# A hybrid decoder block on 8 cores: the causal convolution leaves TensorE, pool sums become scans, gates are taken 1024 wide

## The chip, the cores and the metric

The program runs on the 8 NeuronCores of one Trainium2 chip. Each core computes one batch element of 2048 tokens, alone: the cores exchange nothing. The metric is the device time of the slowest core, in microseconds (us). On each core TensorE (PE), VectorE (DVE), ScalarE (ACT), GpSimd (POOL) and the DMA queues of SyncE (SP) and GpSimd each work in their own order and wait for each other by semaphores.

## What is computed

```python
h = rms_norm(x, norm_mix_pre)
proj = h @ w_in                                  # 1024 -> 4608 columns
x_lru, g_lru, x_pool, gates = split(proj, [1024, 2048, 2560])
# mixer A
x_lru = causal_depthwise_conv(x_lru, conv_w, conv_b)      # 4 taps per channel, along time
r, i = sigmoid(blockdiag(x_lru) + b)                      # 16 heads of 64x64
a = exp(-8 * r * softplus(-lam));  u = sqrt(1 - a*a) * i * x_lru
y_lru = scan(h_t = a_t h_{t-1} + u_t) * gelu(g_lru)
# mixer B, four groups of 128 channels, trailing windows 2, 4, 8, 16
p = mean of the last w tokens - token;  y_pool = (p @ w_grp) * scale
# merge, then the MLP
m = (sigmoid(gate_a) * (y_lru @ w_lru_up) + sigmoid(gate_b) * (y_pool @ w_pool_up)) @ w_o
x = x + rms_norm(m);  x = x + rms_norm(square(relu(rms_norm(x) @ w_ff1)) @ w_ff2)
```

## The kernel before

Channels lie on the 128 partitions and tokens run along the free axis. All of the normed, transposed input of a core is in `hT` (bf16, 8 blocks of 128 channels by 2048 tokens). Tokens are worked in two halves of 1024 (h = 0, 1), and a product is 128 output channels by 512 tokens: 8 matmuls of 128x512 into one of the 8 PSUM banks. The stages:

- A: 16 tiles of 128 tokens are loaded, normed and transposed. The first eight go through TensorE (L598), the other eight through a transposing DMA.
- B: the LRU. The index n runs over 16 channel blocks (8 for each half), and two blocks (n, n+1) are handled together. For each block and each 512 tokens (r = 0, 1): a product for x_lru, cast to bf16 in `xlb` (L733), the convolution, the bias and a cast (L751, L753), two block-diagonal gate matmuls (one of 128x512 each), two tanh, and one multiplication (L760). Then exp, square and sqrt on ScalarE over 1024 tokens, a multiplication (L771), the scan (L773), and the product with the gelu gate (L778).
- C: the pool, one group g at a time: two products, a scaled copy to `xp`, window sums by doubling (L818), the difference (L823). Its weights are folded first on TensorE (L792).
- D2 and D1: the merges of the pool branch (12 matmuls for 512 tokens) and of the LRU branch (16 matmuls), each for 8 output blocks and 2 halves. D1 of a half needs all of B of that half.
- E: w_o, norm, residual; then F1 and F2, the MLP (L921, L976 are matmuls of F2).

The convolution before is `conv_pair` (L709): 16 matmuls of 64x64 by 512 columns for two blocks, 4 taps by 4 quadrants, with the taps as diagonal matrices that GpSimd builds (L692, `conv_diag`). In every second block the two halves of the channels are swapped so that the four quadrants of the array are all in use.

The order on each engine isn't written by hand. Every operation is recorded with a priority, a cost and what it reads and writes; `Prog.schedule` places them one by one, and what comes out is a fixed order for each engine and a fixed place for each PSUM tile. The priorities of the stages come from constants (`PA`, `PC`, `PD2`, ...). Each engine then takes its instructions strictly in that order. GpSimd issues the weight loads (from f32 to bf16 on the way) and may have 4 of them under way: each waits for the one four places ahead. While TensorE has nothing to do in the first 48 us, `fill` puts matmuls on zeros (L1127) into the order, a fixed number in each gap.

`mm` records a group of matmuls (L544), `act` a ScalarE operation (L530), `load` a transfer (L562 on GpSimd's queue, L564 on SyncE's), `merge` one 512-token piece of D1 or D2 (L847 is its product with the gate).

## Time and profile before

| | us |
|---|---|
| Median of 3 runs (lowest 902.21) | 904.66 |
| Span of the profiled execution, slowest core | 901.8 |
| Spans of the eight cores | 896.5 to 901.8 |
| End of TensorE's last matmul, from the span's start | 896.5 |
| TensorE busy | 885.0 |
| VectorE busy | 463.8 |
| ScalarE busy | 369.6 |
| GpSimd busy | 190.7 |

The span is from the first to the last instruction of the slowest core, and the median lies 2.9 us above it. Busy time is a sum over an engine's instructions. Matmuls are pipelined: the mean duration of one (380 ns) is longer than the distance between two, so TensorE's work is counted here by that distance.

### The profile page before, as it was taken

The page shows a single profiled execution, that of the slowest core. Times are in us where ns is not written, and L with a number is a line of the kernel's source. Part 1 is how long each engine was busy: PE and PEld are TensorE (multiplying, and loading weights), DVE is VectorE, ACT ScalarE, POOL GpSimd, SP SyncE. Part 2 cuts the span into 40 slices and gives each one's busy share as a digit, 9 for nine tenths or more (in the row PEclk, how much of TensorE's full clock was granted, in tenths as well). Part 3 has the DMA queues.
Part 4 walks back from the last instruction along what each step waited for, and adds up shares of the span by engine and source line. Part 5 has one row for each costly group of instructions (what it writes and reads, how often), then busy time and mean ns, then how long its engine had stood idle before and what let it go on. Part 6 is the DMA issues. An engine that isn't in the chain of part 4 may idle for free.

```text
span 901.8 us, 13671 instructions; the slowest of 8 cores (896.5 to 901.8 us)
## 1 busy us (share of the span) xinstructions
PE 885.0 (98%) x4462; PEld 408.2 (45%) x4462; DVE 463.8 (51%) x668; ACT 369.6 (41%) x584; POOL 190.7 (21%) x305
## 2 busy tenths in 40 slices
PE   7999999999999999999999999999999999999997
PEld 5544434444444444444444444444444444444444
DVE  5559776984757766675455545111224443312122
ACT  5583867575563673442343334111113333311111
POOL 5323442313130021222233323100001212000000
PEclk9999999999999999999999999999999999999999
DMA  8984697237795399674798999921556555212231
GB/s 211 194 105 59 100 164 100 41 53 106 119 134 71 47 166 209 167 174 121 107 185 137 168 177 152 188 40 24 166 160 108 82 73 80 36 47 76 65 94 47
DMA packets 92870, 102.60 MB, mean 114 GB/s; under 512 B 29313, under 2 KB 80257, under 8 KB 92802
## 3 DMA queue, kind: packets, MB, share of 16 engines
q0 software_dynamic: 52768, 51.78, 42.3%
q1 hardware_dynamic: 40034, 49.96, 22.2%
q8 instruction: 37, 0.61, 0.3%
q14 instruction: 31, 0.25, 0.1%
HBM read 130.43 MB, written 16.78 MB: 163 GB/s over the span
## 4 chain that ended last, share of the span: by engine, by line
PE 92%; DMA 5%; DVE 1%; issue 1%; SPq 0%; DVEq 0%; POOL 0%; ACT 0%; POOLq 0%; ACTq 0%
PE pp L544 66%; PE pp L921 24%; DMA big<-wmrga 2%; DMA big<-wlru 2%; PE pp L709 1%; DMA big<-x 1%; PE pp L976 1%; DVE big L773 0%; PE pp L1127 0%; PE pp L792 0%; SPq L564 0%; DVE big L661 0%; DVE big L771 0%; DVE big L994 0%; PE pp L598 0%
## 5 line engine op out<-in xcount | busy, mean ns | idle before, releaser
L544 PE MATMUL pp<-big 128*128 128x512 bf16 x2880 | 627.9, 380 | 5.7 <-DMA big<-wlru 2.8
L544 PEld LDWEIGHTS pp<-big 128*128 128x128 bf16 x2880 | 280.2, 98 | 349.2 <-issue 17.4
L530 ACT ACTIVATE big<-pp 128x512 f32<-128x512 f32 (+4 forms) x217 | 138.9, 642 | 399.9 <-PE pp L921 185.6
L921 PE MATMUL pp<-big 128*128 128x512 bf16 x992 | 214.4, 379 | 0.0
L910 DVE SCALAR_TENSOR_TENSOR big<-pp,big 128x512 bf16<-128x512 f32 x128 | 88.2, 690 | 127.3 <-ACT big L530 127.2
L921 PEld LDWEIGHTS pp<-big 128*128 128x128 bf16 x992 | 97.1, 98 | 117.0
L530 ACT ACTIVATE big<-pp,dv 128x512 f32<-128x512 f32 x128 | 81.5, 689 | 88.7 <-PE pp L544 59.1
L949 DVE TENSOR_TENSOR big<-pp,big 128x512 f32<-128x512 f32 x31 | 21.3, 691 | 168.9 <-ACT big L530 153.4
L562 POOL DMA_DIRECT2D big<-wff x80 | 59.0, 737 | 212.1 <-PE pp L544 194.0
L530 ACT ACTIVATE big<-big 128x1024 bf16<-128x1024 f32 (+1 forms) x64 | 66.0, 1050 | 21.1 <-DVE big L884 13.5
L847 DVE SCALAR_TENSOR_TENSOR big<-big,pp 128x512 bf16<-128x512 f32 (+1 forms) x64 | 43.0, 682 | 31.0 <-PE pp L544 24.4
L530 ACT ACT_TABLE_LOAD x35 | 44.9, 1283 | 5.0 <-DVE big L609 2.8
L692 POOL TENSOR_SCALAR big<-identb,cvt 128x64 bf16<-128x64 bf16 x64 | 41.5, 674 | 8.0 <-PE pp L709 7.8
L953 POOL TENSOR_SCALAR st<-st 128x1 f32<-128x1 f32 x16 | 3.3, 207 | 160.6 <-ACT big L530 160.6
L773 DVE TENSOR_TENSOR_SCAN big<-big,hcar 128x1024 f32<-128x1024 f32 x16 | 37.0, 2339 | 0.2
L760 DVE SCALAR_TENSOR_TENSOR big<-big 128x512 f32<-128x512 f32 x32 | 22.0, 693 | 23.3 <-ACT big L530 23.3
L570 POOL TENSOR_SCALAR st<-st 128x1 f32<-128x1 f32 x40 | 12.8, 320 | 95.6 <-ACT big L530 94.8
L733 DVE CAST big<-pp 128x512 bf16<-128x512 f32 x32 | 22.0, 688 | 16.7 <-PE pp L544 16.5
L562 POOL DMA_DIRECT2D big<-wmrga x16 | 12.0, 751 | 82.0 <-PE pp L544 64.5
L572 POOL TENSOR_TENSOR st<-st,powc 128x1 f32<-128x1 f32 x40 | 27.4, 684 | 5.8 <-POOL st L570 0.3
L562 POOL DMA_DIRECT2D big<-wlru x18 | 13.9, 773 | 67.1 <-PE pp L544 52.7
L890 DVE SCALAR_TENSOR_TENSOR big<-big,st 128x1024 bf16<-128x1024 f32 x16 | 20.5, 1283 | 13.5 <-POOL st L572 13.4
(71 smaller groups left out, 388.4 us busy)
## 6 DMA issues: line engine op xcount, KB each, us to landing
big<-x SPq DMA_DIRECT2D x32, 512.0 KB, 6.6
big<-wff POOLq DMA_DIRECT2D x64, 256.0 KB, 6.0
big<-wmrga POOLq DMA_DIRECT2D x16, 512.0 KB, 9.4
x1s<-big SPq DMA_DIRECT2D x16, 512.0 KB, 4.7
big<-wff POOLq DMA_DIRECT2D x16, 512.0 KB, 9.8
big<-x1s SPq DMA_DIRECT2D x16, 512.0 KB, 5.0
out<-big SPq DMA_DIRECT2D x31, 256.0 KB, 3.1
big<-wlru POOLq DMA_DIRECT2D x14, 512.0 KB, 9.9
```

The source lines that it names most:

```text
L530: return e.activation(out=o, in_=i, func=func, **kw)
L544: ins = e.matmul(P.bank(tile, k)[:, width], lhsT=lt, rhs=rh, start=(i == 0), stop=(i == len(g) - 1))
L562: return P.add(eng, lambda e: e.dma_start(out=cut, in_=src), reads=list(reads), writes=[dst], dma=name, prio=prio, nbytes=nbytes, after=after)
L572: P.add("pool", lambda e: e.tensor_tensor(out=rs, in0=sd, in1=powc[:, 0:1], op=ALU.pow), reads=[sd, powc[:, 0:1]], writes=[rs], ns=730.0, ...
L692: ins = e.tensor_scalar(out=dst[:, k4, :], in0=identb[:, 128:192], scalar1=cvt[:, col:col + 1], scalar2=None, op0=ALU.mult)
L733: dve(lambda e, R=R, vx=vx, xl=xl: e.tensor_copy(out=xl[:, 3 + R.start:3 + R.stop], in_=P.bank(vx)), [vx], [xl[:, 3 + R.start:3 + R.stop]] ...
L760: dve(lambda e, R=R, xc=xc, I=I: e.scalar_tensor_tensor(out=I[:, R], in0=I[:, R], scalar=1.0, in1=xc, op0=ALU.add, op1=ALU.mult), [I[:, R] ...
L773: dve(lambda e, A=A, I=I, M=M, hc=hc: e.tensor_tensor_scan(out=M, data0=A, data1=I, initial=hc, op0=ALU.mult, op1=ALU.add), [A, I, hc], [M ...
L847: dve(lambda e: e.scalar_tensor_tensor(out=dst, in0=tg, scalar=1.0, in1=P.bank(vb), op0=ALU.add, op1=ALU.mult), [tg, vb], [dst], prio=pr)
L910: dve(lambda e, v=v, o=o, sq=sq: e.scalar_tensor_tensor(out=o, in0=P.bank(v), scalar=0.0, in1=sq, op0=ALU.is_gt, op1=ALU.mult), [v, sq], [ ...
L921: ins = e.matmul(P.bank(v, k0), lhsT=hid[k][:, TS], rhs=wff2[nh][k // 4][:, k % 4, :], start=(k == 0), stop=(k == 31))
L949: dve(lambda e: e.tensor_tensor(out=dst, in0=P.bank(v, k0), in1=gC[:, N], op=ALU.mult), [v, gC[:, N]], [v, dst], prio=pr)
```

## The change

The convolution leaves TensorE. A block's two products for x_lru (1024 tokens) now go to a pair of PSUM banks. ScalarE reads the pair once, with the current token's tap as scale and the bias, and writes `xc` in f32; VectorE then adds the other three taps with three scalar_tensor_tensor (L708 in the changed kernel) that read the same pair shifted by 1, 2 and 3 tokens. In the second half of the tokens three tiny operations add what reaches over the border. The cast of `xc` to bf16 goes to ScalarE for the first block of two and stays on VectorE for the second. The gate matmuls fill a pair of banks, and each tanh and the multiplication behind it is 1024 wide. The pool's windows of 8 and 16 are one running scan each, a window of 2 is one subtraction, and the copy to `xp` is 1024 wide. The very first products are cut into 256 columns. The constants that set the priorities, the order of the first weight loads, and the conditions on the loads are new; loads of the first MLP weights wait for the last x_lru product. The diagonals, `xlb` and the swap of channel halves are gone. The rest of the diff (memoised `cells`, 64-byte granules) concerns the building of the program.

```diff
-    PA = (120.0, 40.37)
-    PC = ((-10.0, 13.83), (424.04, 26.15))
-    PD2 = ((39.35, 81.22), (566.54, 90.4))
-    PD1 = (1065.62, 93.96)
-    PWO = 1125.97
-    PE0 = (1193.64, 24.22)
+    PA = (118.61, 41.34)
+    PC = ((-6.78, 6.03), (429.63, 29.43))
+    PD2 = ((39.63, 81.27), (551.87, 60.4))
+    PD1 = (1079.58, 74.66)
+    PWO = 821.54
+    PE0 = (1079.78, 13.19)
...
+    SPL = 1
+    CAST = (1, 0)
...
-    def conv_diag(n, c):
...
-    def conv_pair(n, vs, R, prio):
...
+    def conv(vx, xc, cc, h, prio):
+        tap = [cvt[:, C_CW + 4 * cc + k:C_CW + 4 * cc + k + 1] for k in range(4)]
+        halo = xhalo[:, 4 * cc:4 * cc + 3]
+        act(xc, lambda: P.pair(vx), AF.Identity, reads=[vx], n=1024, scale=tap[3], bias=cvt[:, C_CONVB + cc:C_CONVB + cc + 1],
+            prio=prio)
+        for d in (1, 2, 3):
+            w = tap[3 - d]
+            dve(lambda e, d=d, w=w: e.scalar_tensor_tensor(out=xc[:, d:H], in0=P.pair(vx)[:, 0:H - d], scalar=w, in1=xc[:, d:H],
+                                                           op0=ALU.mult, op1=ALU.add), [vx, xc, w], [xc], n=1024, ns=1290.0,
+                prio=prio)
+            if h == 1:
+                dve(lambda e, d=d, w=w: e.scalar_tensor_tensor(out=xc[:, 0:d], in0=halo[:, 3 - d:3], scalar=w, in1=xc[:, 0:d],
+                                                               op0=ALU.mult, op1=ALU.add), [halo, xc, w], [xc], ns=160.0,
+                    prio=prio)
...
+    def parts(n, r):
+        return [slice(256 * i, 256 * i + 256) for i in range(2)] if n == 0 and r < SPL else [ALLW]
...
+            conv(vxs[m], xc, cc, h, pg)
+            if CAST[m]:
+                act(xb, xc, AF.Copy, n=1024, prio=pg - 1)
+            else:
+                dve(lambda e, xc=xc, xb=xb: e.tensor_copy(out=xb, in_=xc), [xc], [xb], ns=700.0, prio=pg - 1)
+            for k, dst in ((0, A), (8, I)):
+                v = Ps(2)
+                for r in range(2):
+                    mm([[(wab[:, k + cc, :], xb[:, 512 * r:512 * r + 512])]], [wab, xb], [(v, r, ALLW)], pg - 30, keep=0)
+                act(dst, lambda v=v: P.pair(v), AF.Tanh, reads=[v], n=1024, scale=0.5, prio=pg - 30,
+                    bias=dv[:, D_HBA + k + cc:D_HBA + k + cc + 1])
...
+            dve(lambda e: e.tensor_tensor_scan(out=src[:, 16:HW], data0=xp[:, 16:HW], data1=xp[:, 16 - w:HW - w], initial=sc,
+                                               op0=ALU.add, op1=ALU.subtract), [xp, sc], [src], ns=2290.0, prio=pr)
...
-        stage_F1(0, m, PF1[0] + PF1[1] * m)
+        stage_F1(0, m, PF1[0] + PF1[1] * m, [bmm[-1]])
```

Three places show how the order moves. The first is TensorE at the start, from the sixth group of input transposes (L598 before, L609 after) to the first long stretch of products (L544 before, L555 after); L1127 and L1132 are the matmuls on zeros. Before:

```order
L598 MATMUL pp<-identb,big 128x128 x8
L1127 MATMUL pp<-dull 128x128 x21
L544 MATMUL pp<-big 128x512 x8
L598 MATMUL pp<-identb,big 128x128 x8
L1127 MATMUL pp<-dull 128x128 x7
L709 MATMUL pp<-big 64x512 x16
L598 MATMUL pp<-identb,big 128x128 x8
L1127 MATMUL pp<-dull 128x128 x13
L544 MATMUL pp<-big 128x512 x44
```

The same place after:

```order
L1132 MATMUL pp<-dull 128x128 x45
L609 MATMUL pp<-identb,big 128x128 x8
L1132 MATMUL pp<-dull 128x128 x8
L791 MATMUL pp<-big 128x128 x8
L1132 MATMUL pp<-dull 128x128 x41
L609 MATMUL pp<-identb,big 128x128 x8
L555 MATMUL pp<-big 128x512 x16
L555 MATMUL pp<-big 128x256 x16
L555 MATMUL pp<-big 128x512 x8
L555 MATMUL pp<-big 128x256 x16
```

All eight groups of transposes and the first fold of pool weights (L791) now stand ahead of every product, where two x_lru products and a convolution stood among them.

The second is VectorE while blocks 0 and 1 end and block 2 begins. Before (L771, L773 and L778 end a block, L733 casts an x_lru product, L818, L823 and the lines behind them belong to the pool):

```order
L771 TENSOR_TENSOR big<-big 128x1024
L823 SCALAR_TENSOR_TENSOR big<-big 128x1024 [waits s_dve]
L827 TENSOR_TENSOR big<-big,icnt 128x3
L773 SCALAR_TENSOR_TENSOR big<-big,hcar 128x1024 [waits s_dve]
L829 TENSOR_TENSOR big<-big 128x3 [waits s_dve]
L733 CAST big<-pp 128x512 [waits s_pe]
L803 COPY big<-phalo 128x16 [waits s_dve]
L776 COPY hcar<-big 128x1
L778 SCALAR_TENSOR_TENSOR big<-big 128x1024
L733 CAST big<-pp 128x512 [waits s_pe]
```

After (L770, L772 and L777 are the same three steps, L708 are the three passes of block 2's convolution):

```order
L770 TENSOR_TENSOR big<-big 128x1024 [waits s_act]
L772 SCALAR_TENSOR_TENSOR big<-big,hcar 128x1024 [waits s_dve]
L708 SCALAR_TENSOR_TENSOR big<-pp,cvt,big 128x1023 [waits s_pe,s_act]
L775 COPY hcar<-big 128x1 [waits s_dve]
L777 SCALAR_TENSOR_TENSOR big<-big 128x1024
L770 TENSOR_TENSOR big<-big 128x1024 [waits s_act]
L708 SCALAR_TENSOR_TENSOR big<-pp,cvt,big 128x1022 [waits s_dve]
L772 SCALAR_TENSOR_TENSOR big<-big,hcar 128x1024 [waits s_dve]
L708 SCALAR_TENSOR_TENSOR big<-pp,cvt,big 128x1021 [waits s_dve]
```

The passes of one block's convolution are spread among the last steps of the two blocks ahead of it.

The third is GpSimd's queue around the load of w_o (`wo`; `wmrgb` are weights of D2, `wmrga` of D1, `wlru` of B). Before:

```order
L562 DMA big<-wmrgb 128x3x512 [waits s_pe,d_wmr1]
L562 DMA big<-wmrga 128x4x512 [waits s_pe,d_wmr2]
L562 DMA big<-wo 128x8x512 [waits s_dve,s_act,s_pe,d_wlru2]
L562 DMA big<-wo 128x8x512 [waits d_wlru0]
L562 DMA big<-wmrgb 128x3x512 [waits s_pe,d_wmr0]
```

After:

```order
L573 DMA big<-wlru 128x4x512 [waits s_pe,d_wlru1]
L573 DMA big<-wo 128x8x512 [waits s_dve,s_act,s_pe,d_wlru2]
L573 DMA big<-wo 128x8x512 [waits d_wmr0]
L573 DMA big<-wmrgb 128x3x512 [waits s_pe,d_wlru0]
L573 DMA big<-wmrgb 128x3x512 [waits s_pe,d_wlru1]
L573 DMA big<-wmrgb 128x3x512 [waits s_pe,d_wo0]
L573 DMA big<-wlru 128x4x512 [waits d_wo1,s_pe]
```

The load of w_o, which stood ahead of the last D2 weights, now stands ahead of the weights of the third, fourth and fifth block of the second half's D2.

## Rows read from the trace of the kernel before

**Rows 1.** Page, the chain that ended last, by engine.
```profile
PE 92%; DMA 5%; DVE 1%; issue 1%; SPq 0%; DVEq 0%; POOL 0%; ACT 0%; POOLq 0%; ACTq 0%
```

**Rows 2.** Busy us by stretch: length, PE, PEld, DVE, ACT, POOL, clock, DMA share, GB/s.
```profile
32.50:116.00 83.50, 82.45 (x439) 37.59 (x438) 60.47 (x96) 61.17 (x83) 27.22 (x40) 1.00 0.72 109
116.00:134.00 18.00, 15.91 (x89) 6.18 (x87) 15.71 (x24) 12.03 (x17) 7.91 (x10) 0.91 0.91 166
134.00:350.00 216.00, 215.15 (x1106) 95.07 (x1104) 157.17 (x206) 130.74 (x166) 47.75 (x69) 1.00 0.68 98
...
125.00:130.00 5.00, 5.00 (x19) 1.88 (x17) 4.71 (x7) 3.68 (x6) 1.02 (x2) 0.72 0.32 63
```

**Rows 3.** The chain in order of time: start us, us, what.
```profile
25.75 1.17 PE pp L1127 x21
...
32.46 9.50 PE pp L544 x44
...
44.78 0.45 PE pp L792 x8
...
124.47 8.27 PE pp L544 x30
...
184.88 28.60 PE pp L544 x132
213.48 0.99 PE pp L709 x16
...
564.91 110.51 PE pp L921 x512
```

**Rows 4.** What TensorE waited for: us in total, times, longest.
```profile
PE pp L544 <- DMA big<-wlru: 2.8, 2, 1.7
PE pp L544 <- DVE hcar L776: 2.1, 1, 2.1
```

**Rows 5.** Timeline of ScalarE and of GpSimd near the start.
```profile
23.91 1.06 ACT L530 ACTIVATE big<-big 128x1024 bf16<-128x1024 f32 x1 [0.69 <-DMA big<-x]
...
26.95 0.73 POOL L562 DMA_DIRECT2D big<-wpt  x1
```

**Rows 6.** Groups of instructions: count, busy us, mean ns of one, idle before them.
```profile
L530 ACT ACTIVATE big<-pp,dv 128x512 f32<-128x512 f32 x128 | 81.5, 689 | 88.7 <-PE pp L544 59.1 <-DVE big L850 13.9 <-DVE big L753 6.7
L530 ACT ACT_TABLE_LOAD x35 | 44.9, 1283 | 5.0 <-DVE big L609 2.8 <-DVE warm L633 1.6
...
L773 DVE TENSOR_TENSOR_SCAN big<-big,hcar 128x1024 f32<-128x1024 f32 x16 | 37.0, 2339 | 0.2
...
L751 DVE TENSOR_SCALAR big<-pp,cvt 128x512 f32<-128x512 f32 x32 | 22.8, 744 | 7.4 <-PE pp L709 7.4
L733 DVE CAST big<-pp 128x512 bf16<-128x512 f32 x32 | 22.0, 688 | 16.7 <-PE pp L544 16.5
L760 DVE SCALAR_TENSOR_TENSOR big<-big 128x512 f32<-128x512 f32 x32 | 22.0, 693 | 23.3 <-ACT big L530 23.3
...
L882 DVE SCALAR_TENSOR_TENSOR big<-pp,st,big 128x1024 f32<-128x1024 f32 x16 | 20.5, 1281 | 7.1 <-POOL st L572 7.0
L530 ACT ACTIVATE big<-pp 128x1024 bf16<-128x1024 f32 x20 | 20.5, 1023 | 28.3 <-PE pp L544 27.0 <-PE pp L792 0.9
...
L530 ACT ACTIVATE big<-big,dv 128x1024 f32<-128x1024 f32 x16 | 19.3, 1236 | 0.1
...
L753 DVE CAST big<-big 128x512 bf16<-128x512 f32 x32 | 13.4, 443 | 0.0
...
L818 DVE TENSOR_TENSOR big<-big 128x1024 f32<-128x1024 f32 x8 | 9.7, 1213 | 0.1
```

**Rows 7.** The loads of w_o, and a table load in ScalarE's timeline.
```profile
DMA to landing us min/median/max: 15.4/18.4/21.4
...
112.15 1.28 ACT L530 ACT_TABLE_LOAD   x1
113.45 1.24 ACT L530 ACTIVATE big<-big,dv 128x1024 f32<-128x1024 f32 x1
```

More of the change, by code:

```diff
@@ L698, in build_nc @@
-    LO, HI = slice(0, 64), slice(64, 128)
-    def conv_pair(n, vs, R, prio):
-        srcs = [(n, LO, LO, 0), (n, HI, HI, 0), (n + 1, LO, HI, 1), (n + 1, HI, LO, 1)]
-        def fn(e):
-            ins = None
-            for k4 in range(4):
-                for m, rows, cols, b in srcs:
-                    ins = e.matmul(P.bank(vs[b])[cols], lhsT=convd[m % 4][rows, k4, :],
-                                   rhs=xlb[m % 3][rows, R.start + k4:R.stop + k4], start=(k4 == 0), stop=(k4 == 3))
-            return ins
-        return P.add("pe", fn, reads=[convd[m % 4] for m in (n, n + 1)] +
-                     [xlb[m % 3][:, R.start:R.stop + 3] for m in (n, n + 1)], writes=vs, ns=4 * 264.0 + 60.0, prio=prio,
-                     keep=2)
+                 WLRU[c][2 * k:2 * k + 2], 524288, prio=PW0[2 * n + k], after=x_after(XW[2 * n + k]))
@@ L1035, in build_nc @@
     load_lru(1, 1)
[L1036 removed]
+    load("pool", "wab", wabs, WAB, 524288, prio=PWAB, after=x_after(XW[4]))
     for p in range(2):
```

212 lines of the change are left out of this document (100 added, 112 removed).

## The prediction

> **What bounds the kernel now.** I read four views, in this order. The chain that ended last is TensorE for 92% of the span [rows 1]. The stretches say how full that is: from 32.5 to 350 us, where the changed stages lie, TensorE is busy 313.5 of 317.5 us, VectorE 233.4 (74%) and ScalarE 203.9 (64%) [rows 2]. The chain in order of time gives the price of TensorE's work: 512 matmuls of 128x512 take 110.51 us, 0.2158 us each [rows 3]. A convolution takes 0.99 us, and the 132 matmuls ahead of one take 28.60 us, 0.11 more than 132 x 0.2158, so a convolution costs 1.10 us of TensorE in all [rows 3]. Last, TensorE's waits are few, and two of them carry the loss inside [rows 4].
>
> So the span can be added up. Matmuls of 128x512 (2880 and 992): 3872 x 0.2158 = 835.7. Sixteen convolutions: 17.6. The last output tile (64 matmuls half as wide): 6.9. Eight groups of transposes and four folds of 0.45 [rows 3]: 5.4. Together 865.6 us. By 32.46 us [rows 3] TensorE had done 16 products' matmuls (3.45), eight groups of transposes (3.6) and one convolution (1.1), so 24.3 us went by without useful work. The tail behind the last matmul is 5.3 us. What is left of 901.8 is 6.6 us, lost in the middle. The median of the runs is 2.9 us above this execution, and I add that to each result.
>
> **The change part by part.**
>
> The convolutions leave TensorE: -17.6 us. Nothing else hides them there, since the engine is full. By the Trainium skill ("TensorE: Matmul & The Clock Gate", section "Measured speedup vs the span model") four small matmuls side by side take one matmul's time plus some 4 ns for each further one; as an estimate that makes 0.91 us for the four taps and 14.6 us for sixteen, 3 us less than the rows give. The rows are of this kernel and decide.
>
> Splitting the first products adds 32 instructions, each pair of halves about 3 ns dearer than one whole: +0.1.
>
> The start. All transposes now stand ahead of the first product. The last input tile reaches ScalarE at 23.9 us [rows 5]; square, root and scaling need 3.3 us more, so its transposes could start at about 27.3. But the fold of the first pool weights and 41 matmuls on zeros stand ahead of them. The fold needs three transfers beside the first LRU weights, as many bytes as the four small weight loads of before, three of which had landed when GpSimd issued its next load at 26.95 [rows 5]; I take 26.3. Then 0.45 for the fold, 2.3 for the 41 (21 took 1.17 [rows 3]), 0.45 for the transposes: the first product starts at 29.5 us, with 4.05 us of useful work done. That is 25.45 us without work against 24.3: +1.15. Bounds: 27.5 us (-0.85), if the weights land early, and 32 us (+3.65), if they share the DMA engines badly. The other weights of blocks 0 and 1 are asked for behind these, but the pool's 16 matmuls now run first and give them 3.5 us.
>
> VectorE for one block. Before: two casts of 0.69, two additions of 0.74, two casts of 0.44 and two multiplications of 0.69, 5.1 us. After: three passes over PSUM, for which L882 is the same form (1.28, so 3.84), a cast in every second block (0.44 on average), one 1024-wide multiplication (1.21, by L818): 5.5, and 0.3 for the tiny ones [rows 6]. Sixteen blocks: +10. The pool loses 14 of 20 additions of 1.21 and gains four scans of 2.34: -8 [rows 6]. VectorE's total barely moves, and its share rises with the shorter stretch to 78%. Cost on the path: 0, and 2 us if the three passes wait behind the 2.34 us scans that stand among them. TensorE has five gelu and pool products to do meanwhile.
>
> ScalarE for one block. Before: four tanh of 0.69, 2.76 us. After: the first pass (between 1.02 and 1.24; two per-partition operands, so I take 1.24), two tanh of 1.11, and half a cast of 1.02: 4.0 us [rows 6]. Sixteen blocks: +20. The functions now alternate more often. Following the order of functions, a table has to be loaded 52 times; the same count gives 35 before, which is what the row shows [rows 6]. 17 more of 1.28: +22. The pool's wider copies give 2 back. ScalarE goes from 204 to about 244 us of some 301, 81%. It still has room, so I take 0 on the path; the upper bound is the third rival.
>
> The Trainium skill speaks against this ("ScalarE: Activation LUTs", section "What ACT_TABLE_LOAD costs"): a change of table costs 1.28 us and then a drain of about 1.38. By it the 17 would cost 45 us. The trace doesn't agree: the load at 112.15 ends at 113.43, and the next activation starts at 113.45 [rows 7].
>
> PSUM. A pair of blocks holds four of eight banks from the first x_lru product until the third pass. This is a new hold, priced in the fifth rival.
>
> What moves. The two w_o loads (15.4 and 21.4 us to landing [rows 7]) now stand in GpSimd's queue ahead of the weights of three D2 blocks of the second half. Between the last pool product, which frees their place, and the first product that needs those weights, the changed order has 37 us of TensorE work. The transfers need about 7 us for the pool's end, 21.4 for w_o and 4 for the first D2 weights: hidden, with some 4 us to spare; without that cover a few us. E's and D1's products keep their number, and the first MLP weights have over 100 us after the product that they now wait for: 0. GpSimd loses the diagonals, which were behind no wait of TensorE's: 0.
>
> The middle. Of the 6.6 us lost, 1.1 was a wait for LRU weights (2.8 less the 1.7 at the start) and 2.1 a wait for VectorE [rows 4]. Behind the latter the granted clock fell to 0.72 of full speed for five us [rows 2], and 30 matmuls took 8.27 us in place of 6.5 [rows 3]: 1.8 more. A wait of 2.1 us thus cost 3.9. These belong to the old order, but a new order planned with the same costs has its own. I take 6.6 again, with bounds of 1.5 and 15.
>
> Sum: 865.6 - 17.6 + 0.1 + 25.45 + 6.6 + 5.3 = 885.4 us of span, and with 2.9 a median of 888.3 us, 1.8% below 904.66.
>
> **The rivals.**
>
> 1. Forecast: the convolutions' time and no more. 888.3 us, its own range 885 to 892.
>
> 2. The middle is nearly clean, since other work stands where the waits were. For it: three quarters of the loss hang on two places of the old order, and VectorE keeps its load while the pool's bursts get shorter. Against: fuller ScalarE. 888.3 less 5.3 of the 6.6: 883 us.
>
> 3. ScalarE sets TensorE's pace in parts of B. For it: 81% on average, and in strict order; tanh of gates and merges, which free the banks, queue behind table loads. Against: TensorE has D1 and D2 products between. Two more stalls of the kind seen (3.9 each) give 896 us. The w_o loads, if late, act the same way and are counted here.
>
> 4. Each change of table holds ScalarE twice as long as its row says. Then it gets 22 us more, 266 of 301 (88%), and one stall more than in rival 3: 900 us. The trace speaks against it, as above; the skill's section on table loads is what would bring it about.
>
> 5. Slower than before: the four held banks. If VectorE's three passes come late, TensorE finds no free bank and stops. Each of the eight pairs of blocks can do it. With the clock each such stop costs 3.9, so from five of eight on (19.5 against 16.4 gained) the kernel is slower; with six it takes 912 us. Against: in the order other tiles of one bank go on beside the pairs.
>
> 6. The change doesn't do what it says: the small matmuls ran in time that TensorE can't use otherwise, and it only waits where they were. 904 us. Against: no wait stands beside L709 in the chain.
>
> **How the numbers follow.** Chances: forecast 0.45, rival 2 0.26, rival 3 0.21, rival 4 0.01, rival 5 0.04, rival 6 0.03. A measurement of this kernel can tell about 2% from no change; that limit is 886.6 us. Rival 2 lies below it, and about 0.3 of the forecast's own range: 0.26 + 0.14 = 0.40 for faster by over 2%. Slower by over 2% (above 922.8) needs nearly all pairs to stop: 0.01. Within 2%: 0.59. The range goes from 882, which leaves out the lower third of rival 2 (0.09), to 897, which leaves out the upper part of rival 3 and rivals 4 to 6 (0.11 and a little): 0.2 in all. The predicted time is 888.3.
>
> **What would show it.** In the changed kernel's profile: no L709 matmul; the first long run of products at 29 to 30 us; 52 table loads of 1.28; the group of L708 at 1.28 us; ScalarE near 245 us between 30 and 335; a granted clock of 1.00 there if the waits are short. TensorE's waits show the rest: several for ScalarE of 1 us and more speak for rival 3, for VectorE's L708 for rival 5, for `wmrgb` for late w_o loads, and under 2 us in all for rival 2. I am wrong if the products start past 32 us, if passes over PSUM in place take longer than L882, or if many small waits add up beyond 10 us.

## The result, and the profile after

The changed kernel takes 893.59 us (median of 4 runs, 892.9 to 893.91), the kernel before 904.38 us on the same chip. The ratio is 0.9883, 95% interval 0.9867 to 0.990: 1.2% faster, less than the 2% that I took as the limit. The forecast was 888.3 us with a range of 882 to 897. One of the four executions before (936.19 us), and some in later calls, ran 2.7 to 20% longer with the cores of one die at a lower granted clock, and ratios leave such executions out.

First the page of the changed kernel, slowest core (core 2, span 892.4 us): the chain that ended last, by engine, and three groups that answer to [rows 1] and [rows 6].

```profile
PE 85%; issue 4%; DMA 4%; DVE 3%; ACT 3%; SPq 0%; POOL 0%; DVEq 0%; ACTq 0%; POOLq 0%
...
L708 DVE SCALAR_TENSOR_TENSOR big<-pp,cvt,big 128x1023 f32<-128x1023 f32 (+2 forms) x48 | 60.9, 1277 | 10.4 <-ACT big L541 6.8
L541 ACT ACT_TABLE_LOAD x46 | 59.0, 1283 | 8.4 <-PE pp L555 3.1
...
L541 ACT ACTIVATE big<-pp,cvt 128x1024 f32<-128x1024 f32 x22 | 25.8, 1174 | 25.3 <-PE pp L555 21.9
```

The chain's share of TensorE fell from 92% to 85%: it now runs for 6% of the span over VectorE and ScalarE (1% before), and for another 4% (1% before) over gaps between an event and the next instruction (issue). No small matmul of the convolution is left. The new passes over PSUM cost 1.277 us each (forecast 1.28). The last group mixes the sixteen first passes, 1.19 to 1.21 us each in ScalarE's timeline (forecast 1.24), with six of the pool's copies at 1.09 to 1.11. There are 46 table loads where I had counted 52.

The same stretches as in [rows 2], of the changed kernel (columns as there):

```profile
32.50:116.00 83.50, 78.73 (x405) 38.83 (x412) 64.06 (x79) 66.19 (x76) 16.77 (x25) 1.00 0.72 117
116.00:134.00 18.00, 17.95 (x84) 8.13 (x84) 16.94 (x16) 15.89 (x21) 6.05 (x8) 1.00 0.93 147
134.00:350.00 216.00, 209.46 (x944) 94.47 (x963) 160.42 (x178) 153.39 (x163) 27.44 (x37) 0.98 0.69 102
```

TensorE is busy 306.1 of 317.5 us (313.5 before). ScalarE has 235.5 us of work (203.9 before, forecast about 40 more), VectorE 241.4 (233.4). TensorE, which lost work, stands idle more than it did.

What TensorE waited for, slowest core; the answer to [rows 4]:

```profile
PE pp L555 <- DVE big L854: 4.5, 2, 4.2
PE pp L555 <- ACT big L541: 3.1, 2, 2.1
...
PE pp L555 <- DVE xhalo L716: 2.0, 2, 1.0
```

Where they lie: TensorE's timeline from the first product on (start us, us, instructions, idle before and its releaser).

```profile
29.28 10.89 PE L555 MATMUL pp<-big 128*128 128x512 bf16 x67
...
89.93 3.24 PE L555 MATMUL pp<-big 128*128 128x512 bf16 x14 [1.00 <-DVE xhalo L716]
94.14 17.14 PE L555 MATMUL pp<-big 128*128 128x512 bf16 x76 [0.97 <-ACT big L541]
113.38 27.83 PE L555 MATMUL pp<-big 128*128 128x512 bf16 x126 [2.09 <-ACT big L541]
145.35 36.19 PE L555 MATMUL pp<-big 128*128 128x512 bf16 x153 [4.15 <-DVE big L854]
...
879.76 7.15 PE L983 MATMUL pp<-big 128*128 128x256 bf16 x64
```

The sum can now be read term by term. Useful work is 865.6 - 17.6 + 0.1 = 848.1 us. The first product starts at 29.28 us, with 4.05 us of useful work done: 25.2 us without work (25.45 forecast). The last matmul ends at 886.9, so the tail is 5.5 us (5.3). What is left of 892.4 is 13.6 us, lost in the middle, where I had taken 6.6. The median lies 1.2 us above this span, not 2.9. From 888.3: -0.25, +0.2, +7.0, -1.7 make 893.6. (In each execution of the changed kernels the time is 1.5 to 1.6 us above its own slowest core's span. The rest of my 2.9 was chance: which execution was traced, and a median of three. So 1.7 of the error of 7.0 was made good by luck.) The question is where 13.6 us go.

The two long waits start far away from the engines that TensorE names. The chain of the changed kernel, in order of time (start us, us, what):

```profile
103.06 8.20 DMA big<-x
...
113.38 1.08 PE pp L555 x4
...
124.15 1.28 DVE big L674
125.50 15.33 DMA big<-big
...
142.34 1.13 DVE big L777
143.48 1.14 DVE big L760
144.61 0.61 DVE big L854
...
145.35 6.40 PE pp L555 x18
```

Read it backwards from 145.35. TensorE needs a bank that L854 frees. L854 stands in VectorE's queue behind L760, L777 and a scaling of stage A (L674), and that scaling waits for its buffer, which a transposing DMA holds for 15.33 us. The timeline of VectorE has it in one row:

```profile
141.00 1.28 DVE L674 SCALAR_TENSOR_TENSOR big<-big,st 128x1024 bf16<-128x1024 f32 x1 [6.74 <-DMA big<-big]
```

The wait at 113.38 has the same shape on ScalarE: the square of tile 13 waits 2.69 us for an x tile that takes 8.20 us to land, and the tanh that TensorE needs stands behind it.

```profile
111.40 1.06 ACT L541 ACTIVATE big<-big 128x1024 bf16<-128x1024 f32 x1 [2.69 <-DMA big<-x]
...
112.45 1.25 ACT L541 ACTIVATE big<-pp,dv 128x512 f32<-128x512 f32 x2
```

Then the clock. Stretches of 2 us of the changed kernel (busy us of PE, PEld, DVE, ACT, POOL, granted clock, DMA share, GB/s):

```profile
112.00:114.00 2.00, 0.62 (x3) 0.26 (x4) 0.70 (x2) 1.98 (x5) 1.14 (x3) 1.00 1.23 220
114.00:116.00 2.00, 2.00 (x10) 0.88 (x9) 1.78 (x2) 1.99 (x2) 0.48 (x1) 1.00 1.53 78
...
144.00:146.00 2.00, 0.65 (x2) 0.29 (x3) 2.00 (x3) 0.70 (x2) 0.00 (x0) 0.50 0.95 124
```

Behind the wait of 2.09 us the clock stays at 1.00. In the wait of 4.15 us it falls to 0.50, the lower level of 1.2 GHz, and so it stays until 150 us: 4.65 us of work at half speed, 2.3 us lost. Together: 4.5 + 3.1 + 2.0 of waits, 0.3 for a small one, 2.3 for the clock are 12.2 of the 13.6 us.

All eight cores run the same program, and that is of use here. TensorE waits for L854 for 4.0 to 5.3 us on every core, for L716 2.0 to 2.2, for ScalarE between 1.2 and 3.5. Before, the spans of the eight cores had a mean of 899.5 us, now 890.5. In what follows "middle" is a core's span less 848.1, 25.2 and 5.5, which is 878.8, and its mean over the cores is 11.7 us here. (For the kernel before it is the span less 865.6, 24.3 and 5.3: 4.3 in the mean, 6.6 on the slowest core.)

### The profile page after: what moved, and what is told of

Read it like the earlier page. It is cut to its first block, busy times and chain, and to the rows that moved or that the text cites. A ratio compares the mean times of both kernels' runs of the same rounds, so it can differ in the third digit from the quotient of the medians.

```text
span 892.4 us, 13044 instructions; the slowest of 8 cores (887.7 to 892.4 us)
## 1 busy us (share of the span) xinstructions
PE 867.5 (97%) x4222; PEld 409.4 (46%) x4301; DVE 467.7 (52%) x611; ACT 402.2 (45%) x579; POOL 150.6 (17%) x241
## 4 chain that ended last, share of the span: by engine, by line
PE 85%; issue 4%; DMA 4%; DVE 3%; ACT 3%; SPq 0%; POOL 0%; DVEq 0%; ACTq 0%; POOLq 0%
PE pp L555 60%; PE pp L928 24%; ACT big L541 2%; DMA big<-x 2%; DMA big<-big 2%; PE pp L983 1%; PE pp L1132 1%; DVE big L674 1%; DVE big L826 1%; DVE big L708 0%; ACT L541 0%; DVE big L854 0%; DVE big L830 0%; SPq L575 0%; PE pp L609 0%
## 5 line engine op out<-in xcount | busy, mean ns | idle before, releaser
L555 PE MATMUL pp<-big 128*128 128x512 bf16 (+1 forms) x2853 | 622.8, 378 | 12.9 <-DVE big L854 4.5
L555 PEld LDWEIGHTS pp<-big 128*128 128x128 bf16 x2912 | 284.5, 98 | 349.8 <-issue 18.3
L928 PE MATMUL pp<-big 128*128 128x512 bf16 x972 | 213.4, 379 | 1.1
L928 PEld LDWEIGHTS pp<-big 128*128 128x128 bf16 x992 | 97.1, 98 | 117.0
L541 ACT ACTIVATE big<-big 128x1024 bf16<-128x1024 f32 (+1 forms) x72 | 75.3, 1053 | 55.0 <-DVE big L891 38.5
L541 ACT ACTIVATE big<-pp,dv 128x512 f32<-128x512 f32 (+1 forms) x96 | 76.4, 827 | 40.9 <-PE pp L555 17.7
L708 DVE SCALAR_TENSOR_TENSOR big<-pp,cvt,big 128x1023 f32<-128x1023 f32 (+2 forms) x48 | 60.9, 1277 | 10.4 <-ACT big L541 6.8
L854 DVE SCALAR_TENSOR_TENSOR big<-big,pp 128x512 bf16<-128x512 f32 (+1 forms) x64 | 42.6, 680 | 22.7 <-PE pp L555 14.9
L772 DVE TENSOR_TENSOR_SCAN big<-big,hcar 128x1024 f32<-128x1024 f32 x16 | 37.5, 2346 | 0.6
L541 ACT ACTIVATE big<-pp,cvt 128x1024 f32<-128x1024 f32 x22 | 25.8, 1174 | 25.3 <-PE pp L555 21.9
L573 POOL DMA_DIRECT2D big<-wlru x18 | 13.6, 758 | 114.9 <-PE pp L555 94.0
L581 POOL TENSOR_SCALAR st<-st 128x1 f32<-128x1 f32 x40 | 17.3, 433 | 90.0 <-ACT big L541 89.3
L897 DVE SCALAR_TENSOR_TENSOR big<-big,st 128x1024 bf16<-128x1024 f32 x16 | 20.5, 1284 | 18.7 <-POOL st L583 18.7
L960 POOL TENSOR_SCALAR st<-st 128x1 f32<-128x1 f32 x16 | 3.3, 208 | 151.7 <-ACT big L541 151.6
L760 DVE SCALAR_TENSOR_TENSOR big<-big 128x1024 f32<-128x1024 f32 x16 | 19.5, 1220 | 13.7 <-ACT big L541 13.7
L674 DVE SCALAR_TENSOR_TENSOR big<-big,st 128x1024 bf16<-128x1024 f32 x16 | 20.5, 1282 | 9.1 <-DMA big<-big 6.7
## 6 DMA issues: line engine op xcount, KB each, us to landing
big<-wff POOLq DMA_DIRECT2D x16, 512.0 KB, 10.5
```

The lines of the kernel that those rows point to most:

```text
L541: return e.activation(out=o, in_=i, func=func, **kw)
L555: ins = e.matmul(P.bank(tile, k)[:, width], lhsT=lt, rhs=rh, start=(i == 0), stop=(i == len(g) - 1))
L573: return P.add(eng, lambda e: e.dma_start(out=cut, in_=src), reads=list(reads), writes=[dst], dma=name, prio=prio, nbytes=nbytes, after=after)
L674: dve(lambda e: e.scalar_tensor_tensor(out=hb, in0=xin, scalar=rs, in1=gA1, op0=ALU.mult, op1=ALU.mult), [xin, rs, gA1], [hb], n=1024, pri ...
L708: dve(lambda e, d=d, w=w: e.scalar_tensor_tensor(out=xc[:, d:H], in0=P.pair(vx)[:, 0:H - d], scalar=w, in1=xc[:, d:H], op0=ALU.mult, op1=A ...
L772: dve(lambda e, A=A, I=I, M=M, hc=hc: e.tensor_tensor_scan(out=M, data0=A, data1=I, initial=hc, op0=ALU.mult, op1=ALU.add), [A, I, hc], [M ...
```

## Theories

**Late transfers.** Stage A's second half (tiles 8 to 15) brings transfers whose landing time varies, and each of them is waited for by a queue in strict order, ahead of work that TensorE needs. **ScalarE** (rival 3 of the prediction): table loads and passes set the pace. **Held banks** (rival 5): VectorE's passes over PSUM come late. **The price** (rival 6): TensorE's convolutions did not cost what the sum says.

e2, e4, e5, e6 and e8 leave work out or change it, as said at each, and show only times; the other kernels compute what the reference does. In nearly all kernels below each engine has the order of instructions of the kernel that they are made from; where a dependency is changed, the planner still sees the old one, and only the waits that are written out follow the new one.

## Experiments on the long waits

**A third buffer (e1).** Tiles 8 to 15 use three buffers for the scaled rows, the third in free space.

```
-    hbA = [carve(88 + 2 * s, 2, BF16) for s in range(2)]
+    hbA, trA = [carve(o, 2, BF16) for o in (88, 90, 156)], []
...
-        hb = hbA[tt % 2]
+        hb = hbA[tt % (2 if tt < 8 else 3)]
```

> The changed kernel in its own order of instructions, with one edit: tiles 8 to 15 of stage A write their scaled rows (L674) into one of three buffers in place of one of two. Transfer theory (stage A's transposing DMAs hold the buffers, VectorE waits 6.7 us at L674 with the scan's followers queued behind, TensorE waits 4.2 us and its clock falls): the wait and the slow stretch behind it go, 893.6 less 6 to 7.5 us, about 887 us, and VectorE's longest wait for a big<-big DMA is under 1 us. ScalarE theory (table loads and passes set TensorE's pace): VectorE was early anyway, less than 1.5 us gained, 892 to 894. Held-bank theory (the passes over PSUM come late): 892 to 894 too, and TensorE's wait moves to L708 or L716.

Measured: 889.8 us, ratio 0.9834 (0.9815 to 0.9852), mean of the spans 884.7. The wait for L854 is 0.3 us on seven cores and 0.8 on one. That is the wait that the edit should remove, and neither rival foresaw it. But the time fell by 4, not 6 to 7.5: two cores now lose most at 113 us, where the x tile comes later than in the run above. The slowest core (core 3), the stretch of 2 us behind the wait, and TensorE's waits:

```profile
114.00:116.00 2.00, 2.00 (x7) 0.68 (x6) 2.00 (x3) 1.97 (x3) 0.95 (x2) 0.64 1.22 208
```

```profile
PE pp L555 <- ACT big L541: 3.7, 2, 2.7
```

A wait of 2.7 us here, and the clock falls. The kernel's time is that of its slowest core, so one late x tile on one core is enough.

**No table loads (e2).**

```
-            act(A, A, AF.Exp, n=1024, scale=ch, bias=ch, prio=pc)
+            act(A, A, AF.Exp, n=1024, scale=ch, bias=ch, prio=pc, run=AF.Tanh)
...
-            act(M, M, AF.Sqrt, n=1024, scale=-1.0, bias=1.0, prio=pc)
+            act(M, M, AF.Sqrt, n=1024, scale=-1.0, bias=1.0, prio=pc, run=AF.Square)
```

> The changed kernel in its own order, but the exponentials of stage B run as tanh and its square roots as squares, so that hardly a table is loaded there (other numbers in the output, same tiles). ScalarE theory: some 35 loads of 1.28 us, 45 us of ScalarE's time, go, and with them most of the 13.6 us lost in the middle: 893.6 less 5 to 9, 885 to 889 us. Transfer theory: the loads lie beside TensorE's work, only the 2.1 us wait for ScalarE may shorten since ScalarE has caught up when the late x tile comes; the 4.2 us wait stays: 891 to 893.6 us.

Measured: 889.4 us, ratio 0.9837 (0.9822 to 0.9852), mean span 882.9. The loads fell from 46 to 4:

```profile
L541 ACT ACT_TABLE_LOAD x4 | 5.1, 1283 | 4.6 <-DVE big L620 2.4 <-DVE warm L644 1.6 <-PE pp L555 0.5
```

So 54 us less on ScalarE bought 4 us. The ScalarE theory had asked for 5 to 9. The late-transfer theory as I had put it allowed 2.6 at most: it fell here, in its pure form. The transfers still land late; the row of VectorE below, of core 4, shows a wait of 4.49 us for a transposing DMA, but now for a later tile, and TensorE waits for L854 on three cores only (1.6 to 2.3 us).

```profile
143.67 1.28 DVE L674 SCALAR_TENSOR_TENSOR big<-big,st 128x1024 bf16<-128x1024 f32 x1 [4.49 <-DMA big<-big]
```

**Short passes (e4).** Each pass of VectorE over PSUM covers 64 columns.

```
-... out=xc[:, d:H], in0=P.pair(vx)[:, 0:H - d], scalar=w, in1=xc[:, d:H],
+... out=xc[:, d:d + 64], in0=P.pair(vx)[:, 0:64], scalar=w, in1=xc[:, d:d + 64],
```

> The changed kernel in its own order, but each of the 48 passes of VectorE over a PSUM pair (L708) handles 64 columns in place of some 1022 (part of the convolution is left out). It takes about 1.1 us from each, 50 us of VectorE in all, and frees each pair of banks 3 us earlier. Held-bank theory: TensorE's waits for banks and for the cast go, 893.6 less 5 to 10, 884 to 888 us. Transfer theory: the 4.2 us wait stands behind a DMA that lands when it lands; only the two waits of 1.0 us for the halo copy go: 891 to 892.5 us.

Measured: 890.74 us, ratio 0.9845 (0.9828 to 0.9861), mean span 884.0. 48 us less on VectorE bought 3 us of the median. The waits for L716 fell from 2.0 to 0.6 us, as both theories had it; the wait for L854 is gone on five cores, and on the other three 1.4 to 2.9 us are left. The time lies between the two expectations. What both miss is in the spread of the cores, 879.4 to 889.4 us: on core 5 an x tile took 12.8 us to land and ScalarE waited 4.4 us for it.

**Third buffer and small x (e5).** The x loads of tiles 8 to 15 fetch 128 of 1024 columns.

```
+            q = slice(0, 128 if tt >= 8 else D)
...
-            ... X[tt * 128:(tt + 1) * 128, :], 524288, ...
+            ... dma_start(out=xin[:, q], in_=X[tt * 128:(tt + 1) * 128, q]), ...
```

> The third buffer of the first experiment, and besides the x loads of tiles 8 to 15 fetch 128 columns in place of 1024 (the rest of the tile is stale). Transfer theory: the x tile of 103 us lands early, so ScalarE's 2.7 us wait and with it TensorE's 2.1 us wait goes as well, 2 us under the third buffer alone, about 885 us; of the 13.6 us lost in the middle some 5 are left. ScalarE theory and held-bank theory: 892 to 894.

Measured: 886.19 us, ratio 0.98 (0.9784 to 0.9815), mean span 883.3, and all cores within 2.3 us of each other (882.3 to 884.6). The middle is 4.5 us, as the theory of late transfers had it. On cores 2, 4 and 6 a transposing DMA still took 14.6 to 14.9 us to land: the third buffer keeps that from TensorE, it doesn't make it punctual.

**Small weights, two buffers (e8).** Ten weight loads fetch a quarter of their columns.

```
-            cut, src = rows(dst, src)
+            cut, src = rows(dst, src); c = slice(0, 128 if few else 512)
```

> The changed kernel in its own order and with two buffers as it was, but ten weight loads issued from 87 to 133 us (seven of D2, three of the LRU) fetch a quarter of their columns (the rest is stale). If the transposing DMAs land late because they share the DMA engines with these loads, the landing of 15.3 us falls under 9, the 6.7 us wait at L674 and TensorE's 4.2 us wait go, and the x tile of 103 us lands in time too: 893.6 less 7 to 9, 885 to 887 us. If a transposing DMA is slow by itself or queues behind the others of its kind, the 4.2 us wait stays above 3 and the time above 891.

Measured: 885.86 us, ratio 0.9798 (0.9781 to 0.9815), mean span 883.6, cores within 1.6 us. Nothing of stage A was touched here, no buffer, no order, and both long waits are gone. The landing times of the eight transposing DMAs on the slowest core (least, median, most), first of the changed kernel, then of this one:

```profile
DMA to landing us min/median/max: 2.8/8.0/15.3
```

```profile
DMA to landing us min/median/max: 2.8/5.3/7.1
```

So it is the bytes of ten weight loads under way beside them that make the transfers late (DMA share 1.03 from 100 to 125 us in the changed kernel). That they meet in the DMA engines is the likely reason, but not shown. With a quarter of the bytes the middle is 4.8 us, and the table loads and passes over PSUM are all there.

Taken together: making the transfers punctual (e8), or giving them a buffer and fewer bytes (e5), removes both long waits. Making ScalarE or VectorE emptier (e2, e4) removes some of them, since a queue with slack may have caught up by the time the late transfer holds it; but on three cores of e2 and three of e4 TensorE still waits 1.4 to 2.9 us for L854. Without late transfers neither long wait arises (e8); how full the queue is decides how much of them reaches TensorE. Mean over the eight cores of the traced execution, us, added up from the list of waits of each core:

```
kernel                     L854  ScalarE  L716  wmrgb   mean span  slowest
changed kernel              4.6    2.1     2.0   0.1      890.5     892.4
  once more (e0)            3.6    1.9     2.0   0.0      888.7     890.4
e1 third buffer             0.4    1.8     2.6   0.0      884.7     888.4
e2 no table loads           0.7    1.5     1.6    0       882.9     887.8
e4 short passes             0.8    2.8     0.6    0       884.0     889.4
e5 e1 and small x           0.3    1.2     2.6    0       883.3     884.6
e8 small weights            0.3    1.0     2.7    0       883.6     884.3
e7 e1, cast first           2.8    2.3     0.4    0       885.7     888.3
e12 e7, further             1.0    2.3     0.4    0       883.5     886.7
e10 moved                   2.6    0.3     0.7   1.6      885.3     888.8
e11 moved, loads kept       0.8    0.6     0.6    0       882.1     884.6
```

These executions are of several calls on different chips, and the unaltered kernel differs by 1.8 us between two of them. Over all executions counted, and set against the kernel before in the same call, the mean span fell by 9.6 us (e0), 14.6 (e1), 15.4 (e2), 14.9 (e4), 16.0 (e5), 16.0 (e8), 13.9 (e7), 15.0 (e12), 14.2 (e10), 16.7 (e11) and 10.1 (e9, below).

**The changed kernel again (e0).** The kernel unaltered.

> The changed kernel once more, unaltered, beside the runs of this call: 893 to 894.5 us, 0.988 of the time before. It says how far its time, the 4 us wait and the spread of its cores repeat; the same waits on all eight cores (3.6 to 5.0 us for L854, 2.0 for L716) are expected by every theory.

Measured: 892.67 us, ratio 0.9887 (0.9868 to 0.9906). The time is 0.3 us below the expected range, and so is the wait for L854 on three cores: 1.6, 2.8 and 2.9 us, and 3.6 to 4.8 on the others. It varies with the landing times; the waits for L716 repeat within 0.2 us on every core, as waits that only order makes.

## Experiments on the order

**Cast first (e7).** The remaining waits for L716 have another cause. Ahead of the cast (L753) and the halo copy (L716) stands a multiplication (L770) that only the scan needs. VectorE's timeline of the changed kernel; the halo copy follows at 89.53, and TensorE goes on at 89.93:

```profile
87.79 1.21 DVE L770 TENSOR_TENSOR big<-big 128x1024 f32<-128x1024 f32 x1
88.92 0.68 DVE L753 CAST big<-big 128x1024 bf16<-128x1024 f32 x1
```

```
+ move("dve", mul[2], last[3]); move("dve", mul[6], last[7])
```

(`mul[n]` is L770 of block n, `last[n]` the halo copy of block n.)

> The third buffer of the first experiment, and at two places (blocks 2 and 3, blocks 6 and 7) the multiplication L770 stands behind the cast L753 and the halo copy L716 on VectorE in place of ahead of them. TensorE waited there 1.0 and 1.7 us on every core for the cast and for the held banks. If those waits are the 1.1 us of L770 ahead of the cast, both shrink by 1.1 (to none and 0.6): 889.8 less 2, 887.6 to 888 us. If the three passes themselves are late (held-bank theory), L770 only changes place and the waits stay at 0.8 or more each: 889 to 890.

Measured: 889.63 us, ratio 0.9839 (0.9821 to 0.9857), no gain over e1. The waits for L716 fell from 2.6 to 0.4 us in the mean, as expected, and TensorE waited 2.4 us longer for L854. TensorE's timeline on core 1 (the same wait follows once more at 175.00):

```profile
89.33 2.75 PE L555 MATMUL pp<-big 128*128 128x512 bf16 x12 [1.03 <-DVE big L854]
```

The next thing that TensorE needs is the pair of gate multiplications of D2, and L770 now stood right ahead of those. Neither expectation had that.

**Further back (e12).** L770 goes behind these two as well.

```
+ move("dve", mul[2], mg[0, 8, 1]); move("dve", mul[6], mg[1, 8, 1])
```

(`mg[h, 8, 1]` is the second L854 of D2's block 0.)

> e7 with the two multiplications L770 behind the two gate multiplications of D2 as well. In e7 the waits for the cast fell from 2.7 to 0.6 us and waits of 2.1 us for L854 came in their place, on every core. If order alone is at fault, both are gone now: 889.7 less 2, 887 to 888 us, with ScalarE's wait for a late x tile left on some cores. If VectorE has no room at all around these places, another line takes the 2 us over and it stays at 889 to 890.

Measured: 888.0 us, ratio 0.9833 (0.9817 to 0.985). Of the 2.4 us of new waits 0.6 are left, so they came of order, not of lack of room. In time that shows less: the ratio is e1's (0.9834), and the mean span fell by 15.0 us against e1's 14.6.

**Moved (e10).**

```
+    move("dve", mul[2], last[3])
+    move("dve", mul[6], last[7])
+    back("act", sq[8][0], 4)
+    back("dve", sq[8][1], 5)
+    for tt in (13, 12):
+        back("act", sq[tt][0], 5)
+    for i in (3, 2, 1, 0):
+        back("pool", P.order["pool"][32 + i], 1)
```

(`sq[tt]` holds square and scaling of a tile; `back` puts an instruction so many places later. The squares write into the pool's scratch space in place of the merge gates' buffers.)

> The whole computation, in an order mended at the places that the theory names: third buffer; L770 behind cast and halo copy at two places; the squares of tiles 12 and 13 five places later on ScalarE, so that a tile that lands late holds up no tanh; the square of tile 8 four places later, since it waited 2.4 us for a buffer that it shared with the merge gates, and with other space for what the squares write; the scaling of tile 8 five places later on VectorE. Transfer theory: all eight cores lose less than 4 us in the middle and lie within 2 us of each other: 884 to 886 us. ScalarE theory: the same work in another order, 888 to 890, as the third buffer alone gave.

Measured: 890.23 us, ratio 0.985 (0.9828 to 0.9873). A miss by 4 us, and near what the ScalarE theory expected (888 to 890). ScalarE's waits did go (2.1 to 0.3), but five cores wait 1.0 to 3.4 us for a weight load (`wmrgb`), and all wait 2.4 us for the gate multiplications, as in e7. GpSimd's timeline on core 0 says why; first the changed kernel, then e10:

```profile
90.81 1.39 POOL L581 TENSOR_SCALAR st<-st 128x1 f32<-128x1 f32 x1 [3.20 <-ACT big L541]
...
95.40 0.85 POOL L573 DMA_DIRECT2D big<-wmrgb  x1 [2.15 <-PE pp L555]
```

```profile
95.77 0.89 POOL L601 TENSOR_SCALAR st<-st 128x1 f32<-128x1 f32 x1 [7.32 <-ACT big L561]
...
97.72 0.85 POOL L593 DMA_DIRECT2D big<-wmrgb  x1
```

GpSimd computes the reciprocal root of a tile and issues the weight loads, in one queue. I moved the square of tile 8 back on ScalarE; its root stands ahead of a weight load, so that load went out 2.3 us later. It ran into the next one, issued at 100.94, and that took 13.2 us to land, where none of the four such loads that the changed kernel issues on this core from 90 to 116 us takes more than 11.0. TensorE wanted it at 110.8 and got it at 114.2.

**Moved, loads kept (e11).** Root of tile 8 behind that load, L770 as in e12.

```
-    move("dve", mul[2], last[3])
-    move("dve", mul[6], last[7])
+    move("dve", mul[2], mg[0, 8, 1])
+    move("dve", mul[6], mg[1, 8, 1])
...
-    for i in (3, 2, 1, 0):
-        back("pool", P.order["pool"][32 + i], 1)
+    for i in (35, 34, 33, 32, 22, 21):
+        back("pool", P.order["pool"][i], 1)
```

> The mended order of e10 with two corrections that its trace asks for: the two multiplications L770 stand behind the two gate multiplications of D2 as well (in e10 each stood ahead of them and TensorE waited 1.0 us for these), and the reciprocal root of tile 8 stands behind the next weight load on GpSimd (in e10 the load went out late and TensorE waited 1.0 to 3.4 us for it). By the theory of late transfers and thin slack, 3 to 5 us of waits go: spans of 880 to 883 us on all cores, 883 to 886 us. If VectorE's and ScalarE's amount of work sets the loss, the waits turn up at yet another place: 889 to 891.

Measured: 884.77 us, ratio 0.9795 (0.9779 to 0.9812), mean span 882.1. This kernel computes all that the reference does and is 0.9% faster than the changed kernel (0.9795 by 0.9887 of the same call). TensorE's longest waits on the slowest core (core 4; L877 is L854 in this kernel, L731 is L708):

```profile
PE pp L575 <- DVE big L877: 2.2, 2, 1.6
```

The transposing DMAs are about as late as ever, up to 14.5 us on this core, and the middle is 3.3 us in the mean: on seven cores no wait of TensorE there is above 0.7 us. On core 4 one of 1.6 us is left, at 125.9, and it starts at a late transfer again, an x tile that took 11.93 us to land. ScalarE and VectorE of core 4:

```profile
119.10 1.06 ACT L561 ACTIVATE big<-big 128x1024 bf16<-128x1024 f32 x1 [1.38 <-DMA big<-x]
121.52 1.28 DVE L731 SCALAR_TENSOR_TENSOR big<-pp,cvt,big 128x1023 f32<-128x1023 f32 x1 [3.96 <-ACT big L561]
```

The convolution's first pass stands behind that square on ScalarE, L731 waits for it, and L877 at 125.11 stands behind L731. The kernel has the same amount of work on every engine as e1 and e10 (VectorE 467.7 to 468.0 us, ScalarE 402.2 to 402.6). If the amount of work set the loss, the waits would have turned up elsewhere; they are gone.

## Experiments on the price and the places

**One tap (e6).** The kernel before, with 4 of the 16 small matmuls of each convolution.

```
-            for k4 in range(4):
+            for k4 in range(1):
                 for m, rows, cols, b in srcs:
```

> The kernel before in its own order, its convolution on TensorE cut to one tap of four (4 small matmuls in place of 16; the rest of the convolution is left out). Sixteen times three quarters of 0.99 us are 11.9 us. If TensorE's convolutions lie on the path at the price that the sum gave them, the time falls by 11 to 13 us, to 892 to 894 us. If they ran in time that TensorE can't use otherwise (rival 6), it stays at 903 to 904.6 and TensorE's waits grow by as much.

Measured: 898.11 us, ratio 0.9932 (0.9914 to 0.995), mean span 894.2 against 899.5 (in the mean of the executions of this call 893.8 against 899.5). Both expectations missed. TensorE's timeline of the kernel before, then of e6, around one convolution:

```profile
41.89 1.06 PE L709 MATMUL pp<-big 64*64 64x512 bf16 x16
42.88 1.90 PE L544 MATMUL pp<-big 128*128 128x512 bf16 x8
```

```profile
42.22 0.41 PE L709 MATMUL pp<-big 64*64 64x512 bf16 x4
42.56 1.90 PE L544 MATMUL pp<-big 128*128 128x512 bf16 x8
```

On the engine a convolution fell from 0.99 to 0.34 us, 0.65 and not 0.74: sixteen are 10.4 us. Of these 5.3 to 5.7 arrived. The rest came back as waits: for the cast L753 from 0.7 to 2.5 us in the mean of the cores, for L661 from 1.5 to 2.4, and smaller ones. The time that the convolution took was partly time in which VectorE caught up. In the change, too, the middle grew, from 4.3 to 11.7 us in the mean, with 17.5 us less work. But there it need not: in e11, with as little work on TensorE, it is 3.3. What comes back is a matter of the order, not a fixed share.

**Old places (e9).** The new stage B with the old tables.

```
-    PA = (118.61, 41.34)
+    PA = (120.0, 40.37)
-    PC = ((-6.78, 6.03), (429.63, 29.43))
+    PC = ((-10.0, 13.83), (424.04, 26.15))
...
-    GEARLY = 0.88
+    GEARLY = 1.54
```

> The changed kernel's convolution, scans and gates, but eleven tables of places (stages A, C, D1, D2, E, F1 and the w_o and MLP weight loads) get back the values that they had before the change; those of the start, and those that only the changed stage B has, stay. If the loss in the middle is an accident of one planned order, another order has another loss: anything from 885 to 905 us, with the long waits at other lines than L854 at 145 us. If the loss belongs to the convolution's new work on VectorE and ScalarE (rival theories), it stays near 12 to 14 us and the time at 892 to 896.

Measured: 892.91 us, ratio 0.9879 (0.9858 to 0.99), the same as the changed kernel within what can be told. No core waits for L854 any more. TensorE's timeline on the slowest core:

```profile
145.70 22.61 PE L555 MATMUL pp<-big 128*128 128x512 bf16 x104 [1.78 <-DMA big<-big]
170.14 142.71 PE L555 MATMUL pp<-big 128*128 128x512 bf16 x656 [1.83 <-DVE big L830]
```

The new values of these eleven tables bought nothing that shows; the gain is that of the new stage B. The expectation of "885 to 905" was too wide to test much, and 892.91 fits the rival's 892 to 896 as well; e11 is what tells them apart. What the run does show: another order has its waits elsewhere, one of them again a transposing DMA, and a middle of about the same size (9.3 us in the mean, 9.9 for the changed kernel in the same call). With the old places the slowest of a core's eight transposing DMAs lands after 8.1 to 10.5 us on seven cores (14.1 on one), as it did before the change (9.0 to 10.3), where the changed kernel has 14.8 to 16.2: the very late landings came with the new places, not with the new stage B.

## Why the prediction was right, and where it was wrong

Right were the direction, the range, and the frame: a sum of TensorE's useful work and of the time without it. The time lies outside the 885 to 892 of the forecast proper, though, and nearer to the third rival's 896. Its points in order:

- **The convolutions leave TensorE: -17.6.** Right as work: none of it is left, and nothing else was added. But "Nothing else hides them there, since the engine is full" was wrong as put. e6 took 10.4 us of this work away and got 5.3 to 5.7, and the change kept little more than half; only an order mended by hand (e11) gets nearly all. The estimate of 14.6 us from the Trainium skill ("TensorE: Matmul & The Clock Gate", section "Measured speedup vs the span model") can't be told from 17.6 by these runs.
- **The start: 29.5 us.** Right (29.28).
- **VectorE and ScalarE per block.** Right in size: 1.277 us a pass, +32 us on ScalarE for some 40. I counted 52 table loads, there are 46. The drain behind a load that the Trainium skill states ("ScalarE: Activation LUTs", section "What ACT_TABLE_LOAD costs") was rightly left out: the trace of the changed kernel does not show it either. The load at 113.72 us takes 1.28, and the next activation starts at 115.02.
- **PSUM, fifth rival.** The held banks cost 2.0 us on every core. Its time, 912 us, was far off, its mechanism (VectorE late for cast and halo) was there at two places, for the most part because L770 stood ahead (e7, e12).
- **w_o loads hidden.** Right: no wait for `wmrgb` over 0.5 us on any core.
- **Second rival, 883 us.** A nearly clean middle is possible with this work, as e5, e8 and e11 show (884.8 to 886.2 us); the planned order didn't have it.
- **The step that failed: "The middle ... I take 6.6 again, with bounds of 1.5 and 15."** It was 13.6 us on the slowest core. I had read two waits of the old order and taken them as a sample. I had not asked which transfers a queue in strict order waits for while TensorE's products depend on what stands behind. The trace of before had the rows. On six cores VectorE waits 2.6 to 4.6 us for a transposing DMA, until 112 to 116 us, and on all eight 1.0 to 2.2 us, until 139 to 144. Core 0, and the landing of its eight transposing DMAs, before and then after the change:

```profile
115.44 1.28 DVE L661 SCALAR_TENSOR_TENSOR big<-big,st 128x1024 bf16<-128x1024 f32 x1 [4.55 <-DMA big<-big]
...
DMA to landing us min/median/max: 3.5/7.1/9.8
...
DMA to landing us min/median/max: 2.8/9.2/16.2
```

  Before, at most 1.6 us of that reached TensorE, as waits for the cast L753 on the four cores where VectorE waited longest. The change took slack from the queues and, by its new places, made the latest landings later. e1, e5, e8 and e11 show the mechanism, e2 and e4 what slack does to it.
- **Third rival, 896 us.** Near in time, and right in that waits behind a strict ScalarE queue are part of the loss; wrong in the cause. ScalarE's amount of work does not set the pace: it is 74% busy from 32.5 to 350 us, and e11 has all of it and loses 3.3 us. The sign that I had given for this rival, several waits for ScalarE of 1 us and more, misleads: there are two (2.09 and 0.97 us), and the longer one starts at an x tile.
- **Sixth rival, 904 us.** Wrong as put, since 1.2% was gained, but half of its reasoning holds, as e6 shows.
- **"A wait of 2.1 us thus cost 3.9".** This price, in rivals 3 to 5, was read on one core. In the same execution the same wait for L776 was followed by a fall of the clock on cores 4 to 7 only; so 3.9 us is no fixed price. The 30 matmuls behind it, on core 0 and on core 6:

```profile
122.94 6.63 PE L544 MATMUL pp<-big 128*128 128x512 bf16 x30 [2.09 <-DVE hcar L776]
...
122.01 8.32 PE L544 MATMUL pp<-big 128*128 128x512 bf16 x30 [2.09 <-DVE hcar L776]
```

  On cores 0 to 3 the granted clock is 1.00 from 122 to 130 us, on cores 4 to 6 0.79, on core 7 0.88. (Another wait, of 1.6 and 1.3 us, comes shortly before on cores 4 and 7; none does on 3, 5 and 6.)

Open stays how the 1.4 us of the middle are made up that neither waits nor clock explain, and which of the ten weight loads matters most, which was not tried.

## What to carry to other kernels

When work leaves a full engine, price it as work and then ask what the engines beside it did meanwhile: in e6 half of 10.4 us came back as waits. List every instruction in a strict queue that waits for a DMA, and see what TensorE needs behind it; give it a buffer more, or put it behind the urgent work, and follow its results into every other queue (one weight load behind a moved root cost five cores of e10 up to 3.4 us). Read all cores, since the slowest decides and a late transfer hits one core at a time.

## What was not expected of the hardware

- The same program, the same moment: the wait of ScalarE for the x tile of tile 13 was 0.63 us on core 0 and 3.09 us on core 4 of one execution. On each kernel's slowest core transposing DMAs took 2.8 to 15.3 us to land beside weight loads, 2.8 to 7.1 with a quarter of those bytes (e8).
- The clock. Behind a wait of 2.09 us it stayed at 1.00 (changed kernel, 112 to 120 us). Behind one of 2.41 us it fell; core 0 of e7, stretches of 2 us:

```profile
114.00:116.00 2.00, 2.00 (x8) 0.74 (x7) 1.64 (x2) 1.97 (x3) 0.34 (x1) 0.62 1.51 88
116.00:118.00 2.00, 2.00 (x7) 0.67 (x6) 1.86 (x2) 1.99 (x2) 0.00 (x0) 0.52 1.28 132
```

  From 118 us on it was back at 1.00. The fall cost about 1.7 us, where 0.3 us less of waiting cost none; and in the kernel before a wait of 2.1 us was followed by a fall on four cores and by none on the other four. So the price of a wait near 2 us doesn't follow from its length alone.
- Four small matmuls alone take 0.34 us, sixteen in a row 0.99: the time per small matmul depends on how many stand in a row.
- A pass of ScalarE over a PSUM pair with two per-partition operands takes 1.20 us, less than the 1.24 of the same width from SBUF [rows 6].
